# Mean square of the attention's output made for all partitions by a product with a 128x128 tile, its rstd by POOL on that tile

## The chip, the cores and the metric

One core of a Trainium2 chip. The metric is the device time of one execution of the kernel in microseconds (us), of which the median over runs counts. The engines are PE (TensorE), DVE (VectorE), ACT (ScalarE), POOL (GpSimd) and SP (SyncE, which here issues DMAs).

## What is computed

A decoder layer of 512 tokens and width 1024: one input projection feeds a causal attention (8 heads of 64) and a gated spatial mixer; both results are normalised, joined and sent through an output projection; an MLP and a gated per-layer embedding follow. The change lies in the normalisation of the attention's output.

```python
def rms_norm(x, g):
    xf = x.astype(jnp.float32)
    y = xf * lax.rsqrt(jnp.mean(xf * xf, axis=-1, keepdims=True) + NORM_EPS)
    return (y * g.astype(jnp.float32)).astype(x.dtype)

# in reference():
attn_out = moba_attention(q, k, v)                       # (B, 512, 512)
mixed = jnp.concatenate([rms_norm(attn_out, attn_out_g[i]),
                         rms_norm(gmlp_out, gmlp_out_g[i])], axis=-1)
h = h + rms_norm(jnp.einsum('bse,ed->bsd', mixed, w_o[i]), mix_post_g[i])
```

## The kernel before

Every large product is made of three products of float32 values that are rounded to a high part, with the rest as a low part (`product`, L2700 to L2708: high x high, high x low, low x high). ACT makes the high parts, DVE the low parts by a subtraction. The semaphores are set by hand; each engine executes its instructions in program order, so that an instruction which waits holds back all behind it.

The tokens are worked on in four tiles of 128 (`qt` or `t` from 0 to 3). The attention of a tile runs in units (`UNITS`: one for tile 0, two for tile 1, four for each of tiles 2 and 3). For a unit PE makes the scores (`scores`), DVE adds the causal mask and finds the row maxima (`row_maxima`), ACT takes the exponentials (`softmax`), PE turns the probabilities (`turn_probs`, L2921), DVE and ACT drain the two halves of them (`drain_pt0`, `drain_pt1`), and PE multiplies them with the values (`attend`, L2941) into one bank of PSUM, `BANK_O`. There the output stands turned: channels of a pair of heads on the partitions, tokens along the columns, four pairs beside each other.

When a tile is complete, DVE multiplies it with the turned inverses of the softmax sums into `attn` (`attn_columns`, L1014), and ACT squares it (`square_attn`, L1829). DVE sums the squares of the four pairs into `at_rows`, a tile of 128x128 in SBUF with channels on partitions and tokens along the columns (`attn_sum`, L1021). The mean over channels is a sum over partitions, so PE makes it: `mean_square` (L2800) takes `at_rows` as weights and a column of 1/512 (`mean_of_w`) as data, and gives 128x1: one mean for each token, with tokens on the partitions, in the last columns of `BANK_O`. DVE adds epsilon (`attn_mean`, L1026), POOL raises it to the power -0.5 (`attn_rstd`, L2423), DVE spreads the column to 128 columns of `at_rows` (`attn_spread`, L1031), and PE turns these (`turn_scale`, L2805), so that each partition has the rstd of every token along its columns, in PSUM. DVE multiplies `attn` with it (`attn_scale`, L1038). ACT makes the high part (`attn_hi`, L1834) and DVE the low part (`attn_lo`, L1045) for the output projection.

Between these steps PE works on other products, in an order written by hand: `proj(18)` and `proj(19)` of the value projection, and `proj(20)` to `proj(27)`, which are the output projection, two halves of each tile: `proj(20 + 2 t + half)`. Their channels 4 to 7 (k >= 4) are the attention's, and wait for `attn_lo(t)`. The weights come in slabs: ACT and DVE split them two at a time (`splits`, L1586 and L771), and the first tile of each half waits for each slab. DVE's order in this stage is written at L1093 to L1175, PE's at L2956 to L3027; POOL's is `attn_rstd` 0 and 1, the rstd of projected tile 0 (`out_rstd`) and of the hidden tile 0 (`hidden_rstd`), `attn_rstd(2)`, the same two for tile 1, `attn_rstd(3)`, and then the low parts `hn_lo(0)` and `hn_lo(1)`. After tile 3 the hidden state is normalised and turned (`hn_raw`, `turn_hn`), the products for the per-layer embedding (`ple_tile`) are made and the MLP begins.

`attend` of a tile's first unit waits until `BANK_O` is free, before the change until `attn_scale` of the tile before has been done.

Of the kernel before, what the change touches and what calls it, by code (L numbers as in the profile page):

```python
# [35 lines left out]
ALU = mybir.AluOpType  # L36
# [3 lines left out]
P = 128  # L40
# [4 lines left out]
KD = D // P  # L45
# [270 lines left out]
def hymba_layer(nc, x, xT, pT, weights, columns, rope, ws, rows, out):  # L316
# [6 lines left out]
    with ExitStack() as ctx:  # L323
# [21 lines left out]
        rope_tmp = place("rope_tmp", [P, 2, HEADS, 2 * HALF_ROPE])  # L345
        at_rows = place("at_rows", [P, P], at=at_rope_tmp)
        causal = place("causal", [P, P])
        rope_sb = place("rope_sb", [P, TT, 2, 2 * HALF_ROPE])
        stat = place("stat", [P, 146 + len(GATE_TILES)])
        cols = place("cols", [P, columns.shape[1]])  # L350
        mean_of_w = place("mean_of_w", [P, 1])
        rinv = place("rinv", [P, HEADS])
# [139 lines left out]
        def sem(name):  # L492
# [41 lines left out]
        inverted = sem("inverted")  # L534
        at_rstd, at_spread, scale_filled, at_scaled = (sem("at_rstd"), sem("at_spread"), sem("scale_filled"),
                                                       sem("at_scaled"))
        o_squared, o_rstd, o_gained = sem("o_squared"), sem("o_rstd"), sem("o_gained")
# [217 lines left out]
        def _(dve):  # L755
# [268 lines left out]
            def attn_mean(qt):  # L1024
                dve.wait_ge(mean_filled, qt + 1)
                nc.vector.tensor_scalar(mean_at[:, qt:qt + 1], psum[:, BANK_O, W - P:W - P + 1], EPS, None,  # L1026
                                        ALU.add).then_inc(mean_ready, 1)

            def attn_spread(qt):
                dve.wait_ge(at_rstd, qt + 1)  # L1030
                nc.vector.tensor_copy(at_rows[:], rstd_at[:, qt:qt + 1].to_broadcast([P, P])).then_inc(at_spread, 1)  # L1031

            def attn_scale(qt):

                dve.wait_ge(scale_filled, qt + 1)
                by_pair = attn[:].rearrange("p (a q) -> p a q", a=PAIRS)
                scale = psum[:, BANK_O, W - P:W]
                nc.vector.tensor_tensor(by_pair, by_pair, scale[:, None, :].to_broadcast([P, PAIRS, P]),  # L1038
                                        ALU.mult).then_inc(at_scaled, 1)
# [63 lines left out]
            row_maxima(2)  # L1103
            attn_mean(0)
            attn_spread(0)
            splits(G_O0 * KD + 4)
            splits(G_O0 * KD + 6)
            attn_inverse(1)
            attn_scale(0)
            drain_pt0(1)  # L1110
            drain_pt0(2)
            attn_lo(0)

            attn_columns(1)
            row_maxima(3)
            attn_sum(1)
            row_maxima(4)
            attn_mean(1)
            splits(G_O1 * KD)
            attn_spread(1)  # L1120
            splits(G_O1 * KD + 2)
            attn_scale(1)
            drain_pt0(3)
            drain_pt0(4)
            splits(G_O1 * KD + 4)
            attn_lo(1)
# [15 lines left out]
            attn_mean(2)  # L1142
            attn_spread(2)
            attn_scale(2)
            drain_pt0(7)
            drain_pt0(8)
            attn_lo(2)

# [13 lines left out]
            attn_mean(3)  # L1162
            attn_spread(3)
            gain_mixed(2, 0)
            hn_raw(2)
            hn_raw(3)
            attn_scale(3)
            gain_mixed(2, 1)
# [1154 lines left out]
        def _(pool):  # L2323
            done = [0]

            def after(instruction):
# [14 lines left out]
                                    ).then_inc(constants_set, 1)  # L2341
            nc.gpsimd.memset(mean_of_w[:], 1.0 / W).then_inc(constants_set, 1)
            nc.gpsimd.memset(plus_half, 0.5).then_inc(constants_set, 1)
            pool.wait_ge(constants_set, 5)

# [60 lines left out]
            for i in range(2 * TT):  # L2406
                rotate(i)
                if i == 1:
                    pool.wait_ge(gm_squared, TT)
                    rstd(rstd_gm, ss_gm, W, gm_rstd)  # L2410

            def out_rstd(t):
                pool.wait_ge(o_squared, 2 * t + 2)
                rstd(rstd_o[:, t:t + 1], ss_o[:, 2 * t:2 * t + 1], D, o_rstd,
                     ss_o[:, 2 * t + 1:2 * t + 2])
# [5 lines left out]
            def attn_rstd(qt):  # L2421
                pool.wait_ge(mean_ready, qt + 1)
                nc.gpsimd.tensor_tensor(rstd_at[:, qt:qt + 1], mean_at[:, qt:qt + 1], minus_half[:, 0:1], ALU.pow  # L2423
                                        ).then_inc(at_rstd, 1)
# [272 lines left out]
        def _(pe):  # L2697
# [99 lines left out]

            def mean_square(qt):
                pe.wait_ge(at_summed, qt + 1)
                nc.tensor.matmul(psum[:, BANK_O, W - P:W - P + 1], at_rows[:], mean_of_w[:],  # L2800
                                 start=True, stop=True).then_inc(mean_filled, 1)

            def turn_scale(qt):
                pe.wait_ge(at_spread, qt + 1)
                nc.tensor.transpose(psum[:, BANK_O, W - P:W], at_rows[:], ident[:]  # L2805
                                    ).then_inc(scale_filled, 1)

# [19 lines left out]
            for part in FIRST_RANGES:  # L2829
                for t in range(TT):  # L2830
                    if (t, part) != (0, FIRST_RANGES[0]):
                        proj(t, part)
            pe.wait_ge(constants_set, 5)
            for n in range(TT, 2 * TT):
# [90 lines left out]
            def attend(unit):  # L2925

                qt, pairs = UNITS[unit]
                if unit == 0:
                    pe.wait_ge(*drained["gateT", TT - 1])
                if pairs[0] == 0:  # L2930
                    pe.wait_ge(act_drained, 2 * TT + qt + 1)
                    if qt:
                        pe.wait_ge(attn_ready, qt)
                        pe.wait_ge(at_scaled, qt)
                pe.wait_ge(pt0_drained, unit + 1)
                pe.wait_ge(pt1_drained, unit + 1)
                for j, pair in enumerate(pairs):
                    for k in range(qt + 1):
                        for s in range(2):
                            head = 2 * pair + s  # L2940
                            mm = nc.tensor.matmul(psum[s * DH:(s + 1) * DH, BANK_O, pair * P:(pair + 1) * P],  # L2941
                                                  v[:, k, head * DH:(head + 1) * DH],
                                                  probsT_of[place_in_group(unit)][:, s, j * (qt + 1) + k, :],
                                                  start=(k == 0), stop=(k == qt))
                mm.then_inc(pv_done, 1)
# [13 lines left out]
            scores(2)  # L2959
            proj(18, range(4, KD))  # L2960
            mean_square(0)
            proj(19)
            turn_scale(0)
            turn_probs(1)
# [7 lines left out]
            proj(20, range(0, 4))  # L2972
            mean_square(1)
            proj(20, range(4, KD))
            proj(21, range(0, 1))
            turn_scale(1)
            turn_probs(3)
# [17 lines left out]
            scores(8)  # L2995
            proj(22, range(4, KD))
            mean_square(2)
            proj(23, range(0, 6))
            turn_scale(2)
            turn_probs(7)  # L3000
# [21 lines left out]
            turn_hn(3)  # L3022
            turn_scale(3)
            proj(26, range(0, 4))
# [262 lines left out]
```

## Time and profile before

| what | us |
|---|---|
| median of three runs (578.13 to 578.95) | 578.59 |
| the profiled execution, device time | 578.39 |
| its span, first to last instruction | 576.7 |
| PE busy | 568.4 (99%) |
| DVE busy | 500.4 (87%) |
| ACT busy | 374.9 (65%) |
| POOL busy | 99.3 (17%) |
| granted TensorE clock, mean | 0.996 |

The timelines give for each instruction its start and its duration in us, the engine, the line, and the tiles that it writes and reads with partitions x elements. PE's durations overlap, since products are pipelined; what one costs in PE's order is the distance from its start to the next one's start. In brackets stands how long the engine was idle before and what released it.

### The profile page before, as it was taken

To read this page: it belongs to the slowest core of one execution; us is meant where nothing else is said; L and a number is where in the kernel's file an instruction comes from. 1 tells how busy PE (TensorE), PEld (TensorE's weight loads), DVE (VectorE), ACT (ScalarE), POOL (GpSimd) and SP (SyncE) were. 2 spreads that over 40 slices of the span, in tenths; PEclk is the share of its full clock that TensorE was granted. 3 is DMA by queue.
4 is the path that set the end of the run, shared out by engine and by line. 5 is a ranking of instruction groups with operands and counts; after the bars stand their busy time and mean duration, and the time that the engine had idled before them with its cause. 6 is when DMAs were issued, how large, how long until landed. Compare 5 with 4: busy or idle time off the path is not lost.

```text
span 576.7 us, 8934 instructions
## 1 busy us (share of the span) xinstructions
PE 568.4 (99%) x3364; PEld 496.2 (86%) x3364; DVE 500.4 (87%) x645; ACT 374.9 (65%) x595; POOL 99.3 (17%) x159
## 2 busy tenths in 40 slices
PE   9999999999999999999999999999999999999995
PEld 8888888888888888999999989999998999988884
DVE  5799986688765988999999989999999899798898
ACT  6886774876555746667565565765666656686784
POOL 0332447000102501001010010011010100015122
PEclk9999999999999999999999999999999999999998
DMA  8982008223103597378476394593774753898833
GB/s 271 350 323 83 0 2 315 88 73 110 39 1 110 157 346 226 74 202 202 71 255 148 73 274 91 148 254 43 240 169 82 257 126 79 323 241 173 220 115 148
DMA packets 28603, 93.73 MB, mean 163 GB/s; under 512 B 3216, under 2 KB 4624, under 8 KB 28304
## 3 DMA queue, kind: packets, MB, share of 16 engines
q1 hardware_dynamic: 20736, 67.64, 33.2%
q0 software_dynamic: 5328, 19.14, 19.2%
q10 hardware_dynamic: 2496, 6.37, 2.9%
q8 instruction: 27, 0.44, 0.3%
q14 instruction: 16, 0.13, 0.1%
HBM read 86.85 MB, written 6.29 MB: 162 GB/s over the span
## 4 chain that ended last, share of the span: by engine, by line
PE 87%; DVE 5%; DMA 3%; ACT 2%; issue 2%; POOL 1%; DVEq 0%; ACTq 0%; POOLq 0%
PE psum L2703 27%; PE psum L2707 26%; PE psum L2708 26%; DMA raw_second<-weights_dram 2%; PE psum L2941 2%; PE psum L2758 2%; PE psum L2921 2%; DVE w_lo L1376 1%; DMA raw<-weights_dram 1%; PE psum L2812 1%; DVE h L1486 1%; PE psum L2772 1%; ACT w_hi L2146 1%; DVE psum L1463 1%; DVE psum L1474 0%
## 5 line engine op out<-in xcount | busy, mean ns | idle before, releaser
L2703 PE MATMUL psum<-t_hi,a_hi 128*128 128x512 f32 x216 | 84.7, 392 | 0.0
L2707 PE MATMUL psum<-t_lo,a_hi 128*128 128x512 f32 x216 | 84.6, 392 | 0.0
L2708 PE MATMUL psum<-t_hi,a_lo 128*128 128x512 f32 x216 | 84.0, 389 | 0.0
L2703 PE MATMUL psum<-w_hi,actT_hi 128*128 128x512 f32 (+1 forms) x178 | 69.7, 391 | 0.0
L2708 PE MATMUL psum<-w_hi,actT_lo 128*128 128x512 f32 (+1 forms) x178 | 68.5, 385 | 0.0
L2707 PE MATMUL psum<-w_lo,actT_hi 128*128 128x512 f32 (+1 forms) x178 | 68.4, 385 | 0.0
L2708 PE MATMUL psum<-sum_hi,up_lo 128*128 128x256 f32 x224 | 63.4, 283 | 0.0
L2707 PE MATMUL psum<-sum_lo,up_hi 128*128 128x256 f32 x224 | 63.4, 283 | 0.0
L2703 PE MATMUL psum<-sum_hi,up_hi 128*128 128x256 f32 x224 | 63.2, 282 | 0.0
L2708 PE MATMUL psum<-actT_hi,up_lo 128*128 128x256 f32 (+1 forms) x200 | 60.0, 300 | 0.0
L2707 PE MATMUL psum<-actT_lo,up_hi 128*128 128x256 f32 (+1 forms) x200 | 60.0, 300 | 0.0
L2703 PE MATMUL psum<-actT_hi,up_hi 128*128 128x256 f32 (+1 forms) x200 | 59.9, 299 | 0.0
L2454 POOL DMA_DIRECT2D raw_x<-weights_dram x21 | 18.5, 881 | 237.6 <-DVE t_lo L1235 237.6
L1294 DVE TENSOR_TENSOR acc<-acc,psum 128x512 f32<-128x512 f32 x76 | 49.0, 679 | 1.8 <-PE psum L2708 1.8
L2708 PEld LDWEIGHTS psum<-t_hi,a_lo 128*128 128x128 f32 x216 | 40.6, 188 | 8.9
L1090 DVE TENSOR_TENSOR up_lo<-raw,up_hi 128x1024 fp32r<-128x1024 f32 x37 | 45.1, 1218 | 2.6 <-ACT up_hi L1881 2.0
L2703 PEld LDWEIGHTS psum<-t_hi,a_hi 128*128 128x128 f32 x216 | 40.8, 189 | 7.2
L2707 PEld LDWEIGHTS psum<-t_lo,a_hi 128*128 128x128 f32 x216 | 40.8, 189 | 6.6
L2703 PEld LDWEIGHTS psum<-sum_hi,up_hi 128*128 128x128 f32 x224 | 42.9, 191 | 1.1
L2707 PEld LDWEIGHTS psum<-sum_lo,up_hi 128*128 128x128 f32 x224 | 42.9, 191 | 1.1
L2708 PEld LDWEIGHTS psum<-sum_hi,up_lo 128*128 128x128 f32 x224 | 42.9, 191 | 0.0
L1997 ACT ACTIVATE f<-f 128x512 f32<-128x512 f32 x21 | 13.3, 633 | 41.9 <-DVE f L1230 31.2
(290 smaller groups left out, 1465.7 us busy)
## 6 DMA issues: line engine op xcount, KB each, us to landing
raw<-weights_dram SPq DMA_DIRECT2D x40, 512.0 KB, 4.9
raw_o<-weights_dram SPq DMA_DIRECT2D x23, 512.0 KB, 4.4
raw_x<-weights_dram POOLq DMA_DIRECT2D x21, 512.0 KB, 5.5
raw_second<-weights_dram SPq DMA_DIRECT2D x16, 512.0 KB, 4.0
raw_x<-weights_dram SPq DMA_DIRECT2D x9, 512.0 KB, 6.2
qk_raw<-weights_dram SPq DMA_DIRECT2D x8, 512.0 KB, 6.9
raw_o<-weights_dram POOLq DMA_DIRECT2D x7, 512.0 KB, 7.0
raw_second<-weights_dram POOLq DMA_DIRECT2D x6, 512.0 KB, 6.9
```

The lines of the kernel that those rows point to most:

```text
L1090: nc.vector.tensor_tensor(up_lo[q % UP_SLOTS][:], block_source(step, j), up_hi[q % UP_SLOTS][:].bitcast(F32), ALU.subtract).then_inc(block ...
L1294: nc.vector.tensor_tensor(part, part, bank, how).then_inc(product_added, 1)
L1376: nc.vector.tensor_tensor(gate_half(low, part), gate_source(block, part), gate_half(high, part).bitcast(F32), ALU.subtract).then_inc(block ...
L1463: nc.vector.tensor_tensor(gated_of(i), gated_of(i), ple_of(t)[:, cut], ALU.mult).then_inc(pl_gated, 1)
L1997: nc.scalar.activation(target, source, ACT.Relu).then_inc(relu_done, 1)
L2454: nc.gpsimd.dma_start(raw_x[step % 2][:], weights[down_in_stream(step, rows, half)], accum_op=ALU.add).then_inc(x_added, 16)
L2703: begin = nc.tensor.matmul(out, a_hi, b_hi, start=first, stop=False, skip_group_check=read_between)
L2707: nc.tensor.matmul(out, a_hi, b_lo, start=False, stop=False, skip_group_check=read_between)
L2708: return nc.tensor.matmul(out, a_lo, b_hi, start=False, stop=last, skip_group_check=read_between)
L2758: mm = nc.tensor.transpose(psum[:, banks[name], j * P:(j + 1) * P], source[:, j * P:(j + 1) * P], ident[:])
L2921: mm = nc.tensor.transpose(psum[:, bank + s, k * P:(k + 1) * P], probs[:, place_in_group(unit), s, k * P:(k + 1) * P], ident[:])
L2941: mm = nc.tensor.matmul(psum[s * DH:(s + 1) * DH, BANK_O, pair * P:(pair + 1) * P], v[:, k, head * DH:(head + 1) * DH], probsT_of[place_in ...
```

## The change

For each token tile `mean_square` takes a 128x128 tile filled with 1/512 as weights and `at_rows` as data. The result is 128x128: every partition has the mean of each token along its columns. DVE adds epsilon and writes all of it to `at_rows`, POOL raises the whole 128x128 tile to the power -0.5 in place, and `attn_scale` reads it from there. `attn_spread` and `turn_scale` are gone. `mean_of_w` lies in the second half of the space of `rope_tmp` and is filled after the last rotation. PE's mean product stands directly ahead of the turns of the probabilities for tiles 0 to 2, and between the turns of the hidden state and `proj(25)` for tile 3 as before. DVE's `attn_scale` now stands behind the two drains of the probabilities, or behind `gain_mixed(2, 0)` for tile 3, where it is ahead of `hn_raw(2)` and `hn_raw(3)`. `attend` of the next tile waits for `attn_mean`.

```diff
-        mean_of_w = place("mean_of_w", [P, 1])
+        mean_of_w = place("mean_of_w", [P, P], at=at_rope_tmp + P * 4)
...
             def attn_mean(qt):
                 dve.wait_ge(mean_filled, qt + 1)
-                nc.vector.tensor_scalar(mean_at[:, qt:qt + 1], psum[:, BANK_O, W - P:W - P + 1], EPS, None,
-                                        ALU.add).then_inc(mean_ready, 1)
-
-            def attn_spread(qt):
-                dve.wait_ge(at_rstd, qt + 1)
-                nc.vector.tensor_copy(at_rows[:], rstd_at[:, qt:qt + 1].to_broadcast([P, P])).then_inc(at_spread, 1)
+                nc.vector.tensor_scalar(at_rows[:], psum[:, BANK_O, W - P:W], EPS, None, ALU.add
+                                        ).then_inc(mean_ready, 1)
...
             def attn_scale(qt):
-                dve.wait_ge(scale_filled, qt + 1)
+                dve.wait_ge(at_rstd, qt + 1)
                 by_pair = attn[:].rearrange("p (a q) -> p a q", a=PAIRS)
-                scale = psum[:, BANK_O, W - P:W]
-                nc.vector.tensor_tensor(by_pair, by_pair, scale[:, None, :].to_broadcast([P, PAIRS, P]),
+                nc.vector.tensor_tensor(by_pair, by_pair, at_rows[:, None, :].to_broadcast([P, PAIRS, P]),
                                         ALU.mult).then_inc(at_scaled, 1)
...
             row_maxima(2)
-            attn_mean(0)
-            attn_spread(0)
             splits(G_O0 * KD + 4)
             splits(G_O0 * KD + 6)
             attn_inverse(1)
-            attn_scale(0)
+            attn_mean(0)
             drain_pt0(1)
             drain_pt0(2)
+            attn_scale(0)
             attn_lo(0)
...
             row_maxima(4)
+            splits(G_O1 * KD)
+            splits(G_O1 * KD + 2)
             attn_mean(1)
-            splits(G_O1 * KD)
-            attn_spread(1)
-            splits(G_O1 * KD + 2)
-            attn_scale(1)
             drain_pt0(3)
             drain_pt0(4)
+            attn_scale(1)
             splits(G_O1 * KD + 4)
             attn_lo(1)
...
             attn_mean(2)
-            attn_spread(2)
-            attn_scale(2)
             drain_pt0(7)
             drain_pt0(8)
+            attn_scale(2)
             attn_lo(2)
...
             attn_mean(3)
-            attn_spread(3)
             gain_mixed(2, 0)
+            attn_scale(3)
             hn_raw(2)
             hn_raw(3)
-            attn_scale(3)
             gain_mixed(2, 1)
             attn_lo(3)
...
-                nc.gpsimd.tensor_tensor(rstd_at[:, qt:qt + 1], mean_at[:, qt:qt + 1], minus_half[:, 0:1], ALU.pow
+                nc.gpsimd.tensor_tensor(at_rows[:], at_rows[:], minus_half[:, 0:1].to_broadcast([P, P]), ALU.pow
                                         ).then_inc(at_rstd, 1)
...
-                nc.tensor.matmul(psum[:, BANK_O, W - P:W - P + 1], at_rows[:], mean_of_w[:],
+                nc.tensor.matmul(psum[:, BANK_O, W - P:W], mean_of_w[:], at_rows[:],
                                  start=True, stop=True).then_inc(mean_filled, 1)
-
-            def turn_scale(qt):
-                pe.wait_ge(at_spread, qt + 1)
-                nc.tensor.transpose(psum[:, BANK_O, W - P:W], at_rows[:], ident[:]
-                                    ).then_inc(scale_filled, 1)
...
             proj(18, range(4, KD))
+            proj(19)
             mean_square(0)
-            proj(19)
-            turn_scale(0)
             turn_probs(1)
...
             proj(20, range(0, 4))
-            mean_square(1)
             proj(20, range(4, KD))
             proj(21, range(0, 1))
-            turn_scale(1)
+            mean_square(1)
             turn_probs(3)
...
             proj(22, range(4, KD))
+            proj(23, range(0, 6))
             mean_square(2)
-            proj(23, range(0, 6))
-            turn_scale(2)
             turn_probs(7)
...
             turn_hn(3)
-            turn_scale(3)
             proj(26, range(0, 4))
```

## Rows read from the trace of the kernel before

**Rows 1.** The page: busy time of each engine; the chain by engine.
```profile
PE 568.4 (99%) x3364; PEld 496.2 (86%) x3364; DVE 500.4 (87%) x645; ACT 374.9 (65%) x595; POOL 99.3 (17%) x159
PE 87%; DVE 5%; DMA 3%; ACT 2%; issue 2%; POOL 1%; DVEq 0%; ACTq 0%; POOLq 0%
```

**Rows 2.** Timeline of PE, 118 to 191 us: start, duration, line, tiles.
```profile
118.86 0.28 PE L2800 MATMUL psum<-mean_of_w,at_rows 128*128 128x1 f32 x2
119.00 0.48 PE L2703 MATMUL psum<-w_hi,actT_hi 128*128 128x512 f32 x1
...
124.55 0.27 PE L2805 MATMUL psum<-ident,at_rows 128*128 128x128 f32 x1
124.66 1.91 PE L2921 MATMUL psum<-ident,probs 128*128 128x128 f32 x16
...
133.08 0.48 PE L2703 MATMUL psum<-w_hi,mixT_hi 128*128 128x512 f32 x1
...
135.91 0.39 PE L2703 MATMUL psum<-w_hi,mixT_hi 128*128 128x512 f32 x1
...
143.03 0.39 PE L2703 MATMUL psum<-w_hi,mixT_hi 128*128 128x512 f32 x1
...
190.49 0.39 PE L2703 MATMUL psum<-w_hi,mixT_hi 128*128 128x512 f32 x1
```

**Rows 3.** POOL: groups by line and form (three), then its timeline.
```profile
L2396 POOL TENSOR_TENSOR rope_tmp<-work,rope_sb 128x128 f32<-128x128 f32 x4 | 1.9, 481 | 18.6 <-DVE work L909 17.5 <-ACT work L1726 1.0
L2354 POOL TENSOR_TENSOR stat<-stat 128x4 f32<-128x4 f32 x1 | 1.0, 1028 | 0.1
L2351 POOL TENSOR_TENSOR stat<-stat 128x1 f32<-128x1 f32 x4 | 0.8, 194 | 27.9 <-ACT junk L1620 27.9
...
25.25 0.55 POOL L2354 TENSOR_TENSOR stat<-stat 128x1 f32<-128x1 f32 x1
...
74.03 2.12 POOL L2353 TENSOR_SCALAR stat<-stat 128x4 f32<-128x4 f32 x1
76.23 1.03 POOL L2354 TENSOR_TENSOR stat<-stat 128x4 f32<-128x4 f32 x1
...
120.85 0.56 POOL L2423 TENSOR_TENSOR stat<-stat 128x1 f32<-128x1 f32 x1 [22.19 <-DVE stat L1026]
```

**Rows 4.** Timeline of DVE, 73 to 189 us.
```profile
73.64 2.45 DVE L879 TENSOR_TENSOR w_lo<-qk_raw,w_hi 128x2048 fp32r<-128x2048 f32 x1 [1.95 <-ACT w_hi L1692]
77.29 1.68 DVE L948 TENSOR_SCALAR u<-u,stat 128x512 f32<-128x512 f32 x4 [1.20 <-POOL stat L2354]
...
121.44 0.23 DVE L1031 COPY at_rows<-stat 128x128 f32<-128x128 f32 x1 [0.74 <-POOL stat L2423]
...
125.16 0.68 DVE L1038 TENSOR_TENSOR attn<-attn,psum 128x512 f32<-128x512 f32 x1
...
129.06 0.69 DVE L1014 TENSOR_TENSOR attn<-psum,act_hi_free 128x512 f32<-128x512 f32 x1
...
133.81 1.40 DVE L771 SCALAR_TENSOR_TENSOR w_lo<-raw,cols,w_hi 128x512 fp32r<-128x512 f32 x2
...
143.16 0.42 DVE L979 TENSOR_TENSOR psum<-psum,causal 128x256 f32<-128x256 f32 x1
...
165.62 0.43 DVE L979 TENSOR_TENSOR psum<-psum,causal 128x256 f32<-128x256 f32 x1 [0.98 <-PE psum L2708]
...
188.19 0.68 DVE L1045 TENSOR_TENSOR mixT_lo<-attn,mixT_hi 128x512 fp32r<-128x512 f32 x1
```

**Rows 5.** Timeline of ACT: the high part of tile 0.
```profile
127.58 0.63 ACT L1834 ACTIVATE mixT_hi<-attn 128x512 fp32r<-128x512 f32 x1
```

**Rows 6.** PE's first products (timeline); two stretches: busy by engine, clock, DMA.
```profile
1.12 4.45 PE L2812 MATMUL psum<-warm 128*128 128x128 bf16 x40 [1.12 <-DVE warm L756]
...
565.00:570.00 5.00, 4.50 (x32) 4.03 (x30) 5.00 (x10) 2.69 (x8) 1.51 (x4) 1.00 0.36 136
570.00:577.00 7.00, 0.00 (x0) 0.00 (x0) 4.13 (x9) 0.77 (x4) 1.27 (x4) 0.68 0.54 205
```

More of the change, by code:

```diff
@@ L534, in hymba_layer @@
         inverted = sem("inverted")
-        at_rstd, at_spread, scale_filled, at_scaled = (sem("at_rstd"), sem("at_spread"), sem("scale_filled"),
-                                                       sem("at_scaled"))
+        at_rstd, at_scaled = sem("at_rstd"), sem("at_scaled")
         o_squared, o_rstd, o_gained = sem("o_squared"), sem("o_rstd"), sem("o_gained")
@@ L1025, in attn_mean, with attn_scale @@
                 dve.wait_ge(mean_filled, qt + 1)
-                nc.vector.tensor_scalar(mean_at[:, qt:qt + 1], psum[:, BANK_O, W - P:W - P + 1], EPS, None,
-                                        ALU.add).then_inc(mean_ready, 1)
-            def attn_spread(qt):
+                nc.vector.tensor_scalar(at_rows[:], psum[:, BANK_O, W - P:W], EPS, None, ALU.add
+                                        ).then_inc(mean_ready, 1)
+            def attn_scale(qt):
                 dve.wait_ge(at_rstd, qt + 1)
-                nc.vector.tensor_copy(at_rows[:], rstd_at[:, qt:qt + 1].to_broadcast([P, P])).then_inc(at_spread, 1)
-            def attn_scale(qt):
-                dve.wait_ge(scale_filled, qt + 1)
                 by_pair = attn[:].rearrange("p (a q) -> p a q", a=PAIRS)
-                scale = psum[:, BANK_O, W - P:W]
-                nc.vector.tensor_tensor(by_pair, by_pair, scale[:, None, :].to_broadcast([P, PAIRS, P]),
+                nc.vector.tensor_tensor(by_pair, by_pair, at_rows[:, None, :].to_broadcast([P, PAIRS, P]),
                                         ALU.mult).then_inc(at_scaled, 1)
@@ L2341, in _ @@
                                     ).then_inc(constants_set, 1)
-            nc.gpsimd.memset(mean_of_w[:], 1.0 / W).then_inc(constants_set, 1)
             nc.gpsimd.memset(plus_half, 0.5).then_inc(constants_set, 1)
-            pool.wait_ge(constants_set, 5)
+            pool.wait_ge(constants_set, 4)
             def rstd(target, sums, n, ready, halves=None):
@@ L2410, in _ @@
                     rstd(rstd_gm, ss_gm, W, gm_rstd)
+            nc.gpsimd.memset(mean_of_w[:], 1.0 / W).then_inc(constants_set, 1)
             def out_rstd(t):
@@ L2798, in mean_square @@
             def mean_square(qt):
+                if qt == 0:
+                    pe.wait_ge(constants_set, 5)
                 pe.wait_ge(at_summed, qt + 1)
-                nc.tensor.matmul(psum[:, BANK_O, W - P:W - P + 1], at_rows[:], mean_of_w[:],
+                nc.tensor.matmul(psum[:, BANK_O, W - P:W], mean_of_w[:], at_rows[:],
                                  start=True, stop=True).then_inc(mean_filled, 1)
-            def turn_scale(qt):
-                pe.wait_ge(at_spread, qt + 1)
-                nc.tensor.transpose(psum[:, BANK_O, W - P:W], at_rows[:], ident[:]
-                                    ).then_inc(scale_filled, 1)
             pe.wait_ge(warm_set, 1)
@@ L2832, in _ @@
                         proj(t, part)
-            pe.wait_ge(constants_set, 5)
+            pe.wait_ge(constants_set, 4)
             for n in range(TT, 2 * TT):
@@ L2933, in attend @@
                         pe.wait_ge(attn_ready, qt)
-                        pe.wait_ge(at_scaled, qt)
+                        pe.wait_ge(mean_ready, qt)
                 pe.wait_ge(pt0_drained, unit + 1)
```

## The prediction

> **What bounds the kernel now.** I read the page's busy times first: the tensor engine (PE) is busy 568.4 of 576.7 us, and the chain that ended last is PE for 87% [rows 1]. So the stage of the change (118 to 196 us) is a row of products with hardly a gap, and two things count: what PE no longer issues, and whether anything that PE waits for comes later. The second is found in the timelines: for each step the reader compares the moment an operand is ready with the moment PE takes it. VectorE (DVE) prepares nearly all of PE's operands here, and it executes in program order: an instruction that waits holds everything behind it.
>
> **What PE saves.** `turn_scale` goes: from the start of that turn to the next instruction is 0.11 us (124.55 to 124.66) [rows 2], four times 0.44 us. The mean product stays, with weights and data swapped. Its two passes now stream 128 columns instead of one. In the trace it took 0.14 us of PE's order (118.86 to 119.00) [rows 2]; a 128x128 turn takes 0.11, so two passes take 0.14 to 0.22, and 0.08 more each would leave 0.12 of the 0.44. I take 0.14, since the loading of the weights is already paid in it: -0.44 us, bounds -0.12 and -0.44.
>
> **What DVE saves and pays.** The spread (0.2 us) and the wait for rstd before it go [rows 4]. `attn_mean` reads 128 columns of PSUM instead of one: between the 128x1 form and the 128x512 scale of 0.68 us [rows 4] I take 0.3 us. That is beside PE's work. The memset of 128x128 is on POOL before the stage, long ahead of its use.
>
> **What POOL pays.** This is the term that decides. The power today is 128x1 and takes 0.55 to 0.56 us [rows 3]; afterwards it is 128x128. No row shows one that wide. There is one of 128x4, and it took 1.028 us [rows 3]. Three more columns cost 0.47 to 0.48 us, 0.16 us each. A multiply of 128x128 took 0.48 us [rows 3], so it isn't the reading and writing of 128 columns that costs: it is the power. Carried on, 128 columns take 0.55 + 127 x 0.159 = 20.8 us, or 20.6 with 0.56; I go on with 20.7.
>
> Is 1.03 us the true time of that instruction? POOL's rows vary, and the instruction ahead of it took 2.12 us instead of the usual 0.2. But that one ended at 76.15, as DVE's subtraction of two tiles in SBUF (73.64, 2.45 us) ended at 76.09, and the wide power began at 76.23 with DVE idle until 77.29, which started right as it ended [rows 3, 4]. So nothing on DVE held it. Nor is it first-use cost that I can see: the power at 120.85, 44 us after the one before, took 0.56 [rows 3]. The Trainium skill (SBUF — State Buffer, "SBUF: two separate sides") says that the port pair which VectorE and GpSimd share is an exclusive lock for a whole instruction, where DVE has two SBUF inputs. The trace agrees for the 2.12 us; by that rule the 1.03 us stands undisturbed.
>
> Bounds of the wide power: from below, if the 0.48 us were a one-off, the multiply's 0.48 us plus what a narrow power has over the cheapest of POOL's instructions (0.55 - 0.19) [rows 3], 0.85 us. From above, if all of the 1.03 us is per column and a narrow one has only a costlier start, 128/4 x 0.84 = 27 us (0.84 is 1.03 less the 0.19). I take 20.7 us: it is the straight line through the only two widths.
>
> **Where it lies.** DVE executes mean, two drains, scale, then all later work. Behind the waiting `attn_scale` are queued `attn_lo`, the next `attn_columns`, the row maxima for the next softmax, and the splits of the output weights. I follow each token tile; "shift" is how much later PE is than in the trace. From the end of the power on, scale, high part (ACT) and low part take 0.7 us each [rows 4, 5] with small gaps: 2.1 us until PE may read.
>
> Tile 0. The mean comes after `proj(19)`, near 124.5; DVE adds epsilon near 125.3 and POOL runs from 125.6 to 146.3. `attn_lo(0)` ends at 148.5. PE needed it at 133.08 [rows 2]: it stands still some 15.7 us. Next it needs the first slab of the other half, which DVE splits after the row maxima: `attn_columns(1)` at 148.4 instead of 129.06, so the splits at 153.1 instead of 133.81 (less the mean's 0.1) [rows 4], the slab at 153.9, against 135.91 [rows 2]. Shift 18.0.
>
> Tile 1. DVE's mean at 155.9, POOL 156.2 to 176.9, scale to 177.6, then slab 4 of that half at 178.4; PE wanted it at 143.03 [rows 2], now 161.0. Slab 6 and then the row maxima follow: these start at 180.9 instead of 143.16 [rows 4], 37.75 later, and with the softmax behind them leave PE a shift of 37.2.
>
> Tile 2. POOL 198.4 to 219.1, `attn_lo(2)` 221.2, row maxima 9 at 221.1 instead of 165.62 [rows 4], DVE 55.5 later. The softmax of that unit and its drains were 1.8 us ahead of PE's use, by my reading of the same timelines: shift 53.7.
>
> Tile 3. POOL 236.0 to 256.7. The DVE order is scale, `hn_raw` twice, gain, low part: `attn_lo(3)` starts at 260.55 instead of 188.19 [rows 4], ready at 261.3. PE needed it at 190.49 [rows 2]. DVE is then 72.4 later, and the split of the per-layer input leaves a shift of 71.3. `hn_lo` and the other rstds queued on POOL behind the power are not needed before that.
>
> Sum: 18.0 + 19.2 + 16.5 + 17.6 = 71.3 us, in which PE's own -0.44 vanishes. With its cover gone, a power of X us costs about 4X - 11.5 us.
>
> **The clock.** PE's granted clock was full up to 570 us, and averaged 0.68 over the last 7 us, after its last product at 569.5 [rows 6]. At either full or half, that is 4.5 us at half: it fell some 3 us after work stopped. Four stalls of about 16 us will bring it to 1.2 GHz. The 40 first products took 4.45 us, 0.11 us each [rows 6], the pace of half clock for 128 columns; so a restart loses up to 2.2 us, four 8.8. After tiles 0 and 2 the next wait hides it. I add 3 us, bounds 0 and 8.8.
>
> 578.4 + 71.3 + 3 = 652.7 us in terms of the profiled run (578.39, its span 576.7); the median of the runs is 578.59, so 653.
>
> **Rivals.** (a) The wide power is cheap: the 0.48 us was a one-off and a column costs what a multiply's does, (0.48 - 0.19)/127, 2 ns. The power takes under 1 us and lies beside the two drains of 128x512 (0.6 to 0.7 us each, like the scale [rows 4]), which now stand between mean and scale. The scale then comes at 127.0 instead of 125.16, but ACT takes it at 127.58 anyway [rows 4, 5], and PE's next use has 4 us in hand. The time is 578.59 - 0.44 = 578.2, not slower. It decides below X = 1.8 us or so, the room that the drains leave. For it: 128 partitions are worked on at once whatever the operation, and one row carries the other view. Against it: that row is the only wider power, and undisturbed. The Trainium skill (GPSIMD Engine Reference, "Elementwise — side-by-side cycle accounting") gives about 2.6 cycles an element for GpSimd; by that rule this rival would be right, with an estimate of 0.3 us over the narrow power; the multiply agrees with it, the 128x4 power does not. Chance 0.15, of which 0.03 that DVE's savings bring PE over 1.2 us.
> (b) The slope falls with width, the columns overlapping in POOL's loop: 0.03 to 0.13 us a column, X 4.4 to 17, hence 584 to 637. Nothing shows it but that two widths cannot exclude it. Chance 0.15.
> (c) The cost is 0.21 us a column, X = 27: 578.4 + 4 x 27 - 11.5 + 3 = 678. Chance 0.12.
> (d) My forecast, X from 19 to 22.5, 643 to 664: chance 0.58.
>
> **How the numbers follow.** Forecast 653. The range 605 to 682 leaves out (a), the lower part of (b) and little of (c), together about 0.2. Within 0.2% is about what a measurement can't tell from no change: 577.4 to 579.7. Same 0.12, faster 0.03, slower 0.85.
>
> **What would show it.** The four powers on POOL should have 128x128 and about 20 us each, DVE's `attn_scale` should stand idle before it 18 to 20 us released by POOL, and PE should be idle some 16 us ahead of `proj(20)`'s second half. Half clock should show in short stretches after each stall. If the powers take under 2 us, all of this is wrong and PE shows four turns fewer and nothing else. If they take 20 us but the total is far off 71 us, my order of DVE's queue is wrong.

## The result, and the profile after

The changed kernel takes 652.44 us (median of four runs, 652.31 to 653.18) against 578.36 us (four runs, 578.12 to 578.95): 1.128 times as long, 95% interval 1.1265 to 1.1301. The forecast was 653, range 605 to 682.

From the page of the changed kernel: span and busy times; the chain by engine; the granted clock of PE in the 40 slices of the span; and the group of instructions that now stands first (line, engine, operation, tiles, forms, count | busy us, mean ns | idle before it).

```profile
span 651.5 us, 8922 instructions
PE 578.0 (89%) x3360; PEld 501.7 (77%) x3360; DVE 500.3 (77%) x641; ACT 375.2 (58%) x595; POOL 177.0 (27%) x159
PE 70%; POOL 14%; DVE 8%; DMA 3%; ACT 3%; issue 2%; DVEq 0%; ACTq 0%; POOLq 0%
PEclk9999999968589595799999999999999999999998
L2414 POOL TENSOR_TENSOR at_rows<-at_rows,stat 128x128 f32<-128x128 f32 x4 | 82.9, 20736 | 44.7 <-DVE at_rows L1025 44.7
```

Against [rows 1], DVE and ACT are as busy as before in us; POOL has 78 us more; POOL has gone from 1% of the chain to 14%. One power takes 20.7 us. The clock falls four times in the stage of the change, and else only in the last slice, as before the change.

What PE waits for is in its timeline. These are all its rows with idle time ahead of them in the tiles 0 to 3 (start, duration, then in brackets the idle time before and what ended it):

```profile
148.13 0.79 PE L2694 MATMUL psum<-w_hi,mixT_hi 128*128 128x512 f32 x1 [15.48 <-DVE mixT_lo L1039]
153.73 0.47 PE L2694 MATMUL psum<-w_hi,mixT_hi 128*128 128x512 f32 x1 [0.83 <-DVE w_lo L770]
178.01 0.80 PE L2694 MATMUL psum<-w_hi,mixT_hi 128*128 128x512 f32 x1 [16.82 <-DVE w_lo L770]
221.53 0.79 PE L2694 MATMUL psum<-w_hi,mixT_hi 128*128 128x512 f32 x1 [13.84 <-DVE mixT_lo L1039]
262.73 0.79 PE L2694 MATMUL psum<-w_hi,mixT_hi 128*128 128x512 f32 x1 [18.23 <-DVE mixT_lo L1039]
```

The first, third, fourth and fifth are tiles 0 to 3. They answer to 133.08, 143.03 and 190.49 in [rows 2] (tile 2's is not shown there). All name DVE, which is only the last link. DVE's own timeline shows what it waited for; tile 0:

```profile
124.84 0.28 DVE L1025 TENSOR_SCALAR at_rows<-psum 128x128 f32<-128x128 f32 x1
125.05 0.68 DVE L993 COPY probsT<-psum 128x512 f32<-128x512 f32 x1
125.71 0.69 DVE L993 COPY act_hi_free<-psum 128x512 f32<-128x512 f32 x1
145.99 0.69 DVE L1032 TENSOR_TENSOR attn<-attn,at_rows 128x512 f32<-128x512 f32 x1 [19.59 <-POOL at_rows L2414]
147.38 0.69 DVE L1039 TENSOR_TENSOR mixT_lo<-attn,mixT_hi 128x512 fp32r<-128x512 f32 x1 [0.69 <-ACT mixT_hi L1824]
148.21 0.69 DVE L1013 TENSOR_TENSOR attn<-psum,act_hi_free 128x512 f32<-128x512 f32 x1
```

The reader is to see the 19.59 us: mean and drains are done by 126.4, and then the engine that feeds PE stands still for POOL, with the next tile's `attn_columns` (129.06 in [rows 4], now 148.21) queued behind the wait. DVE stood 76.8 us behind POOL in the four tiles, and PE's idle time ahead of its products is the 65.2 us above. PE's busy time rose by 9.6 us (568.4 to 578.0), because its products run at half clock after each stall, and 65.2 + 9.6 is the whole difference of 74.8 us between the spans. The 9.6 us are not what the clock costs, though: at full clock PE would have reached its next wait sooner, and waited longer there. What the clock costs is measured below.

### The profile page after: what moved, and what is told of

It is laid out like the page before. It is cut to its first block, busy times and chain, and to the rows that moved or that the text cites. A ratio compares the mean times of both kernels' runs of the same rounds, so it can differ in the third digit from the quotient of the medians.

```text
span 651.5 us, 8922 instructions
## 1 busy us (share of the span) xinstructions
PE 578.0 (89%) x3360; PEld 501.7 (77%) x3360; DVE 500.3 (77%) x641; ACT 375.2 (58%) x595; POOL 177.0 (27%) x159
## 4 chain that ended last, share of the span: by engine, by line
PE 70%; POOL 14%; DVE 8%; DMA 3%; ACT 3%; issue 2%; DVEq 0%; ACTq 0%; POOLq 0%
PE psum L2694 22%; PE psum L2698 22%; PE psum L2699 22%; POOL at_rows L2414 13%; DMA raw_second<-weights_dram 2%; PE psum L2749 1%; DMA raw<-weights_dram 1%; DVE w_lo L1366 1%; DVE w_lo L770 1%; PE psum L2927 1%; DVE stat L982 1%; PE psum L2798 1%; PE psum L2907 1%; DVE attn L1032 1%; DVE h L1476 1%
## 5 line engine op out<-in xcount | busy, mean ns | idle before, releaser
L2414 POOL TENSOR_TENSOR at_rows<-at_rows,stat 128x128 f32<-128x128 f32 x4 | 82.9, 20736 | 44.7 <-DVE at_rows L1025 44.7
L2694 PE MATMUL psum<-w_hi,mixT_hi 128*128 128x512 f32 x64 | 30.2, 472 | 65.2 <-DVE mixT_lo L1039 47.5
L2694 PEld LDWEIGHTS psum<-w_hi,mixT_hi 128*128 128x128 f32 x64 | 14.2, 222 | 71.5 <-DVE mixT_lo L1039 48.8
L1032 DVE TENSOR_TENSOR attn<-attn,at_rows 128x512 f32<-128x512 f32 x4 | 3.8, 956 | 76.8 <-POOL at_rows L2414 76.8
```

The source lines that it names most:

```text
L1032: nc.vector.tensor_tensor(by_pair, by_pair, at_rows[:, None, :].to_broadcast([P, PAIRS, P]), ALU.mult).then_inc(at_scaled, 1)
L2414: nc.gpsimd.tensor_tensor(at_rows[:], at_rows[:], minus_half[:, 0:1].to_broadcast([P, P]), ALU.pow).then_inc(at_rstd, 1)
L2694: begin = nc.tensor.matmul(out, a_hi, b_hi, start=first, stop=False, skip_group_check=read_between)
```

## The experiments

The times of one group of runs share the runs of the kernel before on the same chip.

**The power or everything else (a_mult).** One word changed:

```diff
-                nc.gpsimd.tensor_tensor(at_rows[:], at_rows[:], minus_half[:, 0:1].to_broadcast([P, P]), ALU.pow
+                nc.gpsimd.tensor_tensor(at_rows[:], at_rows[:], minus_half[:, 0:1].to_broadcast([P, P]), ALU.mult
```

> The changed kernel with POOL's power replaced by a multiply of the same two operands (so the output isn't normalised; all else is in place: the order, the 128x128 product, the waits). My theory, that only the arithmetic of the power costs: POOL's instruction takes 0.46 to 0.5 us, PE never stands still, and the time is that of the kernel before less the four turns, 578.36 - 0.44 = 577.9 us. Rival 1, the new order of DVE's queue or the wait for POOL costs in itself: over 600 us. Rival 2, the exponent read with a stride of zero or the 128x128 shape makes POOL slow whatever the operation: POOL's instruction still takes about 20 us and the time stays at 652.

Measured: 578.03 us against 578.46, ratio 0.9987, interval 0.9979 to 0.9996. POOL's row in tile 0, from its timeline:

```profile
126.33 0.40 POOL L2414 TENSOR_TENSOR at_rows<-at_rows,stat 128x128 f32<-128x128 f32 x1 [26.77 <-DVE at_rows L1025]
```

PE has no idle row left in the stage. Both rivals fall: order, waits, shape and the exponent's zero stride cost nothing that shows, the power costs all 74 us. So this is also about the most that the change could bring with a free power: 0.1%.

The term that the loss had covered, PE's saving of 0.44 us, fits the medians (-0.43 us), but they can't fix it: the interval runs from 0.2 to 1.2 us. PE's own order can. From the first place where the two orders differ to the first product of `ple_tile` it takes 77.07 us in the kernel before (118.86 to 195.93) and 76.50 in a_mult (119.68 to 196.18), so 0.57 us are saved. The mean product directly ahead of the turns takes 0.22 us, at the upper end of what the prediction allowed:

```profile
125.12 0.38 PE L2793 MATMUL psum<-at_rows,mean_of_w 128*128 128x128 f32 x2
125.34 1.91 PE L2907 MATMUL psum<-ident,probs 128*128 128x128 f32 x16
```

In exchange the products behind it are no longer held up: `proj(19)` took 5.55 us behind the mean product (119.00 to 124.55) and takes 5.44 now (119.68 to 125.12). The sum had no term for that.

**How the price grows with width (a_widths, a_half).**

```diff
-                nc.gpsimd.tensor_tensor(at_rows[:], at_rows[:], minus_half[:, 0:1].to_broadcast([P, P]), ALU.pow
+                n = (8, 16, 32, 64)[qt]          # a_half: 64 in all four
+                nc.gpsimd.tensor_tensor(at_rows[:, 0:n], at_rows[:, 0:n], minus_half[:, 0:1].to_broadcast([P, n]),
+                                        ALU.pow
```

> The changed kernel with the power on the first 8, 16, 32 and 64 columns in tiles 0, 1, 2 and 3 (the other columns stay without it). My theory, a straight line from the first column: 1.66, 2.9, 5.5 and 10.6 us. Rival, columns worked on in blocks: steps, so that 8 costs as much as 16 or the line doesn't go through 0.55 us at one column. The time by my slacks (1.5 to 4.2 us a tile) is 578 + 0 + 1.3 + 1.3 + 7.5 = about 588 us.

POOL's timeline in a_widths:

```profile
125.38 1.67 POOL L2415 TENSOR_TENSOR at_rows<-at_rows,stat 128x8 f32<-128x8 f32 x1 [26.51 <-DVE at_rows L1025]
136.96 2.90 POOL L2415 TENSOR_TENSOR at_rows<-at_rows,stat 128x16 f32<-128x16 f32 x1 [9.92 <-DVE at_rows L1025]
161.43 5.42 POOL L2415 TENSOR_TENSOR at_rows<-at_rows,stat 128x32 f32<-128x32 f32 x1 [6.66 <-DVE at_rows L1025]
183.86 10.53 POOL L2415 TENSOR_TENSOR at_rows<-at_rows,stat 128x64 f32<-128x64 f32 x1 [1.63 <-DVE at_rows L1025]
```

Each doubling adds 0.154 to 0.160 us a column: (2.90 - 1.67)/8, (5.42 - 2.90)/16, (10.53 - 5.42)/32, and (20.74 - 10.53)/64 with the changed kernel's. Expected were 1.66, 2.9, 5.5 and 10.6. A straight line, no blocks. (The comment in the edit above stands for a_half's own edit.) The kernel took 590.0 us in its one execution, where 588 was worked out.

> The changed kernel with the power on the first 64 of 128 columns only (the other columns stay without it). My theory, a straight line by columns: 0.55 + 63 x 0.159 = 10.6 us for one power, and by my sum 4 x 10.6 - 11.5 = 31 us more than 578.4, with 0 to 4 us for the clock: 609 to 613 us. Rival, blocks or a cost that falls with width: the power is clearly off 10.6 us (5 us or less, or 14 or more). Rival, the cost of a stall is not linear in the power's length because the slack of tiles adds up differently: under 600 us or over 620.

Measured 612.65 us, ratio 1.0582 (1.0565 to 1.06). The last of its four powers:

```profile
206.97 10.53 POOL L2414 TENSOR_TENSOR at_rows<-at_rows,stat 128x64 f32<-128x64 f32 x1 [1.63 <-DVE at_rows L1025]
```

My sum gives 4 x 10.53 - 11.5 = 30.6 us, the measured difference is 34.2. The other 3.6 us are not all of the clock: from PE's restart in tile 3 to the first product of `ple_tile` it takes 8.28 us (223.08 to 231.36), 2.8 more than the 5.44 before the change (0.5 of which the sum has as a wait), and DVE's scale of tile 3 took 1.74 us here too, which is 1.05 us that the sum does not have (see b_late).

**What the price is by (a_forms).** Tile 0: a full tile of exponents; tile 1: a multiply; tile 2: half of the partitions; tile 3: four instructions of 32 columns.

```diff
+                if qt == 0:
+                    nc.gpsimd.tensor_tensor(at_rows[:], at_rows[:], mean_of_w[:], ALU.pow).then_inc(at_rstd, 1)
+                elif qt == 1:
+                    nc.gpsimd.tensor_tensor(at_rows[:], at_rows[:], minus_half[:, 0:1].to_broadcast([P, P]), ALU.mult
+                                            ).then_inc(at_rstd, 1)
+                elif qt == 2:
+                    nc.gpsimd.tensor_tensor(at_rows[0:64, :], at_rows[0:64, :],
+                                            minus_half[0:64, 0:1].to_broadcast([64, P]), ALU.pow).then_inc(at_rstd, 1)
+                else:
+                    for c in range(4):
+                        part = nc.gpsimd.tensor_tensor(at_rows[:, 32 * c:32 * c + 32], at_rows[:, 32 * c:32 * c + 32],
+                                                       minus_half[:, 0:1].to_broadcast([P, 32]), ALU.pow)
+                    part.then_inc(at_rstd, 1)
```

> The changed kernel with four forms of POOL's instruction: tile 0 the power with a full 128x128 tile of exponents (all 1/512 instead of -0.5, so tile 0 isn't normalised), tile 1 a multiply (not normalised), tile 2 the power on 64 of the 128 partitions (the other half stays without it), tile 3 the power in four instructions of 32 columns. My theory, the price is by column and by nothing else: 20.7 us, 0.40 us, 20.7 us, and four of 5.4 us. Rival 1, the broadcast exponent is slow: tile 0 is much shorter than 20.7 us. Rival 2, the price is by element: tile 2 takes 10.5 us. Rival 3, a long instruction is slower than short ones: tile 3 takes clearly less than 21 us in all.

POOL's timeline:

```profile
125.41 20.80 POOL L2415 TENSOR_TENSOR at_rows<-at_rows,mean_of_w 128x128 f32<-128x128 f32 x1 [26.38 <-DVE at_rows L1025]
156.12 0.40 POOL L2417 TENSOR_TENSOR at_rows<-at_rows,stat 128x128 f32<-128x128 f32 x1 [9.90 <-DVE at_rows L1025]
179.78 20.73 POOL L2420 TENSOR_TENSOR at_rows<-at_rows,stat 64x128 f32<-64x128 f32 x1 [6.67 <-DVE at_rows L1025]
217.55 21.57 POOL L2424 TENSOR_TENSOR at_rows<-at_rows,stat 128x32 f32<-128x32 f32 x4 [1.68 <-DVE at_rows L1025]
```

None of the three rivals holds. Half the partitions cost the same 20.73 us: the price is by column, and a full tile of exponents of another value costs 20.80 us. The kernel took 635.19 us in its one execution. And four short instructions cost 0.8 us more than one long one, not less.

**What the clock costs (a_fill, b_fill3).** Products whose results are never read were put ahead of PE's waits, so that the granted clock stays up. The edit shown is b_fill3's; a_fill has such a loop at three places, as its comment says:

```diff
             proj(27, range(0, 4))
+            pe.wait_ge(mean_ready, TT)
+            for _ in range(310):             # a_fill: 220 here, 240 in tile 0, 260 in tile 1
+                nc.tensor.matmul(psum[:, BANK_O, 0:P], warm[:], warm[:], start=True, stop=True)
             proj(26, range(4, KD))
```

> The changed kernel with products that have no use (128x128 of bf16, results never read) put into PE's order ahead of the waits of tiles 0, 1 and 3: 240, 260 and 220 of them, 12 to 14.5 us at full clock, so that PE is idle there for 2 to 5 us at most instead of 15 to 18. My theory, that the half clock after a stall costs about 3 us of the 74 in tiles 1 and 3: the granted clock stays at 1.0 after these stalls and the time is 649 to 650 us. Rival, that the half clock lies beside other waits: no change, 652.4. Rival, that it costs more than I put down (8.8 us): 644 us.

Measured 653.31 us: no gain. The windows of two stretches (span, busy us by engine, then the granted clock, DMA share, GB/s), first of the changed kernel, then of a_fill:

```profile
160.00:178.00 18.00, 1.20 (x6) 0.62 (x4) 1.40 (x3) 0.67 (x2) 16.57 (x1) 0.66 0.00 0
178.00:190.00 12.00, 11.99 (x70) 9.68 (x72) 9.56 (x18) 5.88 (x16) 0.95 (x3) 0.81 0.25 89
```

```profile
160.00:178.00 18.00, 17.75 (x286) 16.71 (x282) 1.02 (x2) 0.30 (x1) 16.95 (x1) 1.00 0.01 2
178.00:190.00 12.00, 10.53 (x72) 7.92 (x74) 10.02 (x20) 6.24 (x17) 0.94 (x3) 1.00 0.25 89
```

And a_fill's next wait in PE's timeline:

```profile
185.31 0.87 PE L2907 MATMUL psum<-ident,probs 128*128 128x128 f32 x6 [0.64 <-ACT probs L1797]
```

In tile 1 the clock stayed full, PE was through its products sooner, and then waited for the softmax (185.31, in the changed kernel 185.09). So most of the half clock of tile 1 lay beside DVE's and ACT's work. Not all of it: from the end of POOL's power of tile 1 to the start of that of tile 2 it takes 21.57 us in a_fill (176.94 to 198.51) and 22.06 in the changed kernel (176.57 to 198.63), so 0.5 us were on the path. The traces in which DVE and POOL have the same order in between give this distance for half clocks of other lengths (read from the granted clock behind PE's restart):

| run | half clock in tile 1, us | power 1's end to power 2's start, us |
|---|---|---|
| a_fill | 0 | 21.57 |
| b_fill3 | 3.1 | 21.57 |
| c_after | 4.5 | 21.96 |
| b_late | 4.6 | 22.02 |
| the changed kernel | 4.6 | 22.06 |
| c_both | 6.0 | 22.72 |

About 3 us of half clock are hidden, and what goes beyond is paid. Such small amounts don't show in a_fill's median. In tile 3 the 220 products ended 5.9 us too early and the clock had fallen again: nothing was tested there. Hence the second:

> The changed kernel with 310 products that have no use (bf16, 128 columns, never read) ahead of PE's wait in tile 3 only, 17.6 us at full clock, since in a_fill the 220 ended 5.9 us before PE could go on and the clock fell all the same. My theory now: only tile 3's half clock is on the path (PE's products of 512 columns stood 0.43 us apart instead of 0.23 for the first 5.3 us after the stall), so that it costs 2.3 us: 652.4 - 2.3 = 650.1 us, with granted clock 1.0 from 262.7 us on. Rival, DVE behind it bounds that stretch too: no change, 652.4.

The products behind the stall of tile 3 in the changed kernel, where PE resumes at 262.73, and then in b_fill3 (PE's timeline):

```profile
263.32 0.63 PE L2698 MATMUL psum<-w_lo,mixT_hi 128*128 128x512 f32 x1
263.75 0.63 PE L2699 MATMUL psum<-w_hi,mixT_lo 128*128 128x512 f32 x1
...
268.24 0.39 PE L2698 MATMUL psum<-w_lo,mixT_hi 128*128 128x512 f32 x1
...
270.75 0.39 PE L2694 MATMUL psum<-w_hi,pT_hi 128*128 128x512 f32 x1
```

```profile
262.47 0.50 PE L2694 MATMUL psum<-w_hi,mixT_hi 128*128 128x512 f32 x1 [0.91 <-DVE mixT_lo L1039]
262.80 0.39 PE L2698 MATMUL psum<-w_lo,mixT_hi 128*128 128x512 f32 x1
...
268.50 0.47 PE L2694 MATMUL psum<-w_hi,pT_hi 128*128 128x512 f32 x1 [0.28 <-issue]
```

At half clock the starts are 0.43 us apart, from 268 us on 0.23. From the restart to the first product of the per-layer input it takes 8.0 us instead of 6.0: 2.0 us are on the path in tile 3 in this execution. At full clock it is still 0.6 more than the 5.44 us of the kernel before. The median was 652.21, ratio 1.1277, too close to 652.44 to show it.

**The scale that took 1.75 us (b_late).** In the changed kernel's tile 3, DVE's scale and POOL's `hn_lo(0)` are both released by the end of the power. DVE's row in its timeline, and POOL's:

```profile
257.17 1.75 DVE L1032 TENSOR_TENSOR attn<-attn,at_rows 128x512 f32<-128x512 f32 x1 [18.10 <-POOL at_rows L2414]
```

```profile
257.10 2.94 POOL L2428 TENSOR_TENSOR actT_lo<-xr,actT_hi 128x512 fp32r<-128x512 f32 x2
```

```diff
             attn_rstd(3)
+            pool.wait_ge(at_scaled, TT)
             hn_lo(0)
```

> The changed kernel with one more wait on POOL: hn_lo(0) is started only after DVE's last attn_scale (in the changed kernel's trace both start at 257.1 and 257.2 us, and the scale takes 1.75 us instead of 0.69). My theory, that DVE's instruction with two tiles in SBUF stands behind POOL's: the scale takes 0.69 us again, and as it is on the path, 652.4 - 1.0 = 651.4 us. Rival, the scale's 1.75 us lies beside ACT's work: it takes 0.69 us but the time stays at 652.4. Rival, it has another cause: it still takes 1.75 us.

The same row of DVE's timeline in b_late, and PE's next one:

```profile
257.33 0.69 DVE L1032 TENSOR_TENSOR attn<-attn,at_rows 128x512 f32<-128x512 f32 x1 [18.10 <-POOL at_rows L2414]
```

```profile
261.84 0.80 PE L2695 MATMUL psum<-w_hi,mixT_hi 128*128 128x512 f32 x1 [17.19 <-DVE mixT_lo L1039]
```

The scale takes 0.69 us again and PE's stall is 17.19 instead of 18.23 us: 1.04 us, on the path. The span of this execution was 2.1 us shorter (649.4), though; the other 1.1 us were luck. Its half clock in tile 3 lasted only 2.9 us instead of 5.3, and the first product of the per-layer input came 6.90 us behind the restart instead of 8.02:

```profile
268.74 0.39 PE L2695 MATMUL psum<-w_hi,pT_hi 128*128 128x512 f32 x1
```

The median was 651.64; since single executions lie 1 us apart, the two small effects were measured together against the changed kernel on one chip:

> Both edits of b_late and b_fill3 together: POOL's hn_lo(0) waits for the last attn_scale, and the products without use keep PE's clock up ahead of its wait in tile 3. Theory, from the profiles of the two (PE idle 1.04 us less; the 24 products behind the stall done 2.0 us sooner, and the rest of the kernel 368.1 us long in each): the two add up, 3 us less than c_after in the same rounds, 649.3 to 650. Rival, their medians (651.6 and 652.2) are right and the two profiled executions were lucky: 651 to 652 us, no clear difference from c_after.

> The changed kernel once more, unaltered, on the same chip as c_both and in as many rounds, since single executions of it lie 1 us apart and the effects of b_late and b_fill3 are 1 and 2 us: 652 to 653 us, ratio 1.128.

Measured: c_both 651.39 us (651.14 to 651.89), c_after 653.02 (652.44 to 653.3). The two ranges don't touch, so there is a gain, but of 1.6 us, not of 3. In the profiled executions these rows, c_after's first and then c_both's, bound the stretch that was changed:

```profile
257.12 1.75 DVE L1032 TENSOR_TENSOR attn<-attn,at_rows 128x512 f32<-128x512 f32 x1 [18.10 <-POOL at_rows L2414]
270.69 0.39 PE L2694 MATMUL psum<-w_hi,pT_hi 128*128 128x512 f32 x1
```

```profile
258.57 0.69 DVE L1032 TENSOR_TENSOR attn<-attn,at_rows 128x512 f32<-128x512 f32 x1 [18.10 <-POOL at_rows L2414]
269.10 0.47 PE L2695 MATMUL psum<-w_hi,pT_hi 128*128 128x512 f32 x1 [0.29 <-issue]
```

It has shrunk from 13.57 to 10.53 us, by the full 3.0, but the spans are only 1.1 us apart (651.3 and 650.2; this was the slowest of c_both's five executions). 1.45 us were lost ahead of the stretch, where nothing was changed. 0.50 of them arose before the first of the four powers starts (125.77 against 125.27). 0.76 arose in tile 1, where the half clock lasted 6.0 us instead of 4.5, and 0.2 in tile 2. Another 0.5 us were lost behind the stretch. Why the medians are 1.6 us apart and not 3 is open. Part of it may be that without the filling products the half clock of tile 3 is sometimes as short as in b_late, and then costs 1 us and not 2; the executions without a trace can't show it.

**Does POOL's long instruction shut DVE out (a_lock)?**

```diff
             splits(G_O1 * KD)
+            attn_mean(1)
             splits(G_O1 * KD + 2)
-            attn_mean(1)
```

> The changed kernel with DVE's mean of tile 1 ahead of the second pair of splits instead of behind it; those splits read two tiles in SBUF (raw and high part) and now fall into POOL's power. Theory A, POOL holds the port pair that both use for its whole instruction: the first split is done only 20 us later, when the power ends, both drains follow it, and PE, which waits for the drains, works on 4 us of products after the stall instead of before it: 654 to 656 us. Theory B, POOL's long power leaves the port free between its columns: the splits take their usual 1.4 us for two, beside the power, which starts 1.3 us earlier for it: 651 us.

DVE's timeline, then POOL's:

```profile
155.13 0.29 DVE L1025 TENSOR_SCALAR at_rows<-psum 128x128 f32<-128x128 f32 x1 [0.68 <-PE psum L2793]
155.34 1.55 DVE L770 SCALAR_TENSOR_TENSOR w_lo<-raw,cols,w_hi 128x512 fp32r<-128x512 f32 x2
```

```profile
155.50 21.16 POOL L2414 TENSOR_TENSOR at_rows<-at_rows,stat 128x128 f32<-128x128 f32 x1 [9.34 <-DVE at_rows L1025]
```

Theory A falls: the two splits took 1.55 us instead of 1.41, in the midst of the power, which became 0.44 us longer (20.72 in the changed kernel). The time, 653.13 us, is not B's 651 either: the power began only 0.35 us earlier than in the changed kernel (155.85), since the mean now waited for PE, and that was used up by its being longer: it ended at 176.66 against 176.57.

## Why the prediction was right

**The term that decides** was right: 20.7 us by a line through 128x1 and 128x4, 20.74 measured. What carried it was to ask whether the single row of 128x4 was disturbed [rows 3, 4]; all five widths measured since lie on its line. The question was not idle: of the 128x1 powers of line L2354 in the same trace, whose usual time is 0.55 us, five took 0.94 to 1.54, and one row like these would have given a line far off.

**The path.** The four shifts of PE, forecast and measured, at four places of the two traces:

| place | before | after | shift | forecast |
|---|---|---|---|---|
| tile 0: `proj(21)`'s first product | 135.91 | 153.73 | 17.8 | 18.0 |
| tile 1: `attend(5)` | 149.89 | 187.18 | 37.3 | 37.2 |
| tile 2: `proj(25)`'s first product | 177.31 | 231.25 | 53.9 | 53.7 |
| tile 3: first product of `ple_tile` | 195.93 | 270.75 | 74.8 | 71.3, and 3 for the clock |

The spans differ by 651.5 - 576.7 = 74.8 us, so all of it arises up to there and nothing is given back later: the MLP and the gate need as long as before. In tile 1's 37.3 the 0.5 us of the clock are contained, which the forecast beside it does not have.

**Tile 3 is where terms were mis-sized,** and they nearly cancel, which is luck: what was too small comes to 1.4 us, what was too large to 0.9. PE resumes at 262.73 instead of the forecast 261.3: 0.4 us because the power began later, 1.06 because the scale was held up by `hn_lo(0)`. I had looked only at who needs `hn_lo`, not at what it shares with the scale that starts at the same moment. The wait of 0.5 us that I had put behind it, for the split of the per-layer input, didn't show, since PE was slower by then; in b_fill3, at full clock, 0.6 us more than before the change are there.

**The clock.** The row at the kernel's end gave the mechanism, and PE did run at 1.2 GHz after each stall. 3 us were put down in all; in the profiled execution tile 3 shows 8.02 us for what took 5.44 us before, 2.6 more, of which filling PE took back 2.0 (b_fill3), and tile 1 has 0.5. That most of tile 1 is hidden was not forecast (I had named tiles 0 and 2, where nothing shows), so the total is about right and its distribution partly wrong. The estimate of 2.2 us for a restart was a little low for this execution: the first products of tile 3 stayed 0.43 us apart for 5.3 us, of which 46% are lost, 2.5 us.

**What PE saves** was put at 0.44 us, four turns of 0.11. The traces show 0.57, and the parts differ from the sum's: the mean product did grow, to 0.22 us, and the products behind it no longer lose 0.11. It decides nothing here.

**The rivals.** (a), the cheap power, is refuted by the widths, and its figure of 578.2 us is what a free one would give (578.03 in a_mult). (b) and (c) fall with the straight line. The Trainium skill (GPSIMD Engine Reference, "Elementwise — side-by-side cycle accounting") gives about 2.6 cycles an element, by an estimate with the page's 1.2 GHz 0.28 us for 128 columns. That fits the multiply (0.40 us in all); for the power, 0.16 us a column, it misses by a factor of some 73.

## What to carry to other kernels

On POOL, price an operation by its columns and by what it computes: a power costs 0.16 us a column, as much on 64 partitions as on 128, so values that are the same for all partitions are raised while they are one column, and spread afterwards. Before widening an operation to save a turn of 0.11 us, find a second width in the trace, check what ran beside it, and draw the line. An engine that waits in program order multiplies a long instruction elsewhere: list what is queued behind the wait and when its consumer wants it; the stall is the length less that room, here (4 x 20.7 - 71.3)/4 = 2.9 us a tile by the forecast. Measured it is 2.7: 82.9 us of powers, 74.8 us of shift, 2.6 of them in tile 3 behind the restart.

## What the runs showed of the hardware

- POOL's power of 128x128 took 20.74 us (a_forms: of 64x128 just as long, 20.73), and a multiply of 128x128 0.40 us (a_mult).
- DVE and POOL disturb each other, but not for the length of an instruction in all cases. DVE's scale took 1.75 us behind POOL's `hn_lo`, and 0.69 with `hn_lo` held back (b_late). In the other direction there is only a coincidence in the trace: POOL's `tensor_scalar` of 0.2 us ended with DVE's subtraction, after 2.12 us [rows 3, 4]. But two splits with two tiles in SBUF passed beside a power of 21 us with 0.14 us lost (a_lock). The Trainium skill (SBUF — State Buffer, "SBUF: two separate sides") lets whichever starts first keep the shared pair for the whole instruction. By that rule the splits would have ended after the power; the measurement decides against it for this instruction. Why a power lets them pass and a subtraction holds the scale up, no run shows. DVE's copies from PSUM took their usual 0.68 us beside the power.
- PE's half clock after a stall (granted clock 0.50) lasted differently in executions with the same work behind the stall: in tile 3 2.9 us in b_late and 5.3 in the changed kernel, in tile 1 4.5 us in c_after and 6.0 in c_both. In tile 3 the 2.4 us are 1.1 us of time, which is about the scatter between single executions of a kernel with stalls; that it is the whole cause of the scatter was not shown.
